# Attention steps in another order: VectorE's low part of the probabilities ahead of the maximum, ScalarE's high part ahead of the exponential

## The chip, the cores and the metric

The kernel runs on one core of a Trainium2 chip. The metric is the device time in microseconds (us) of one execution. TensorE (PE) multiplies matrices, VectorE (DVE) and ScalarE (ACT) work on elements and read PSUM banks, GpSimd (POOL) works on elements in SBUF, SyncE (SP) starts the transfers of the weights. Each engine runs its own instructions in the order in which they are written, and waits on semaphores for the others.

## What is computed

Two transformer blocks of two layers each, over 512 tokens of width 1024, in float32. The change is in the attention of the first block, which runs once in each of its two layers. There are 8 heads of grouped-query attention and 8 of latent attention (MLA). For each head:

```python
sc = jnp.einsum('bqhgd,bkhd->bhgqk', qblk, k).astype(jnp.float32) * scale
p = jax.nn.softmax(sc, axis=-1).astype(v.dtype)
return jnp.einsum('bhgqk,bkhd->bqhgd', p, v)
```

The queries and keys of an MLA head come from a small product of a latent vector, part of which is turned by a rotary embedding.

## The kernel before

Every float32 operand of a product is held as a high part (rounded to fp32r, names that end in H) and a low part (the rest, names that end in L), and each product is three matmuls: high by high, low by high, high by low (lines 1800, 1801 and 1802, in a helper). A matmul over 512 columns takes TensorE some 0.23 us from start to start.

The program is a list of steps. A planner appends them in order, and then each engine goes through the whole list and issues its own part of every step. So the order in the list is the order on every engine, and a step in which an engine has no part costs it nothing.

`attention_steps` writes the attention as a pipeline of 72 turns x. A unit is a tile of 128 queries of one head, 4 to a head, so 64 units a layer. In turn x the list holds these steps:

- att_scores of unit x: TensorE's scores (into bank 2 or 3), VectorE's negated row maximum (STAT<-bank, line 1494), ScalarE's exponential with its row sum (TMP<-bank, line 1174);
- att_normalise of unit x-1: VectorE's reciprocal of the sum (line 1499), GpSimd's multiplication of the 128x512 tile by it (line 883);
- att_transpose of unit x-3: four TensorE transposes (line 1961, into bank 4 or 5), ScalarE's high part of the transposed probabilities (PGH or PHH<-bank, line 1180);
- att_values: TensorE's product with the values, of a head whose four units are done;
- att_lo of unit x-4: VectorE's low part of the transposed probabilities (PGL or PHL<-bank, line 1388);
- then the steps that prepare the next heads (`latents`, turn_in, turn_high, turn_rest, turn_sine, turn_out, turn_low, mla_mm, mla_evac, mla_k, mla_v).

What ties the steps together: the transposes of unit x-3 wait for GpSimd's tile of x-3 and for the low part of unit x-5, which frees their bank. The scores of unit x wait for the exponential of x-2. The product with the values waits for the low parts of all four units of its head.

The preparation of an MLA head takes four turns (called phases here, after `(x + 2) % 4`). Phase 2: GpSimd multiplies by the cosine (FF<-FF, line 862) and cuts the key (MKL, line 873), after ScalarE's RH (line 1153) and MKH (line 1164). Phase 3: VectorE makes RL<-FF,RH (line 1388). Phase 0: TensorE turns it (lines 1915, 1916), VectorE multiplies by the sine (line 1475), GpSimd adds (FF<-FF, line 869), and TensorE makes the next head's product (mla_mm). Phase 1: ScalarE cuts MQH (line 1157) and VectorE MQL<-FF,MQH (line 1388), and for a head further on ScalarE makes MVH (line 1168) and VectorE MVL (line 1388). The rows call FF what is the tile of the head being prepared.

Of the kernel before, what the change touches and what calls it, by code (L numbers as in the profile page):

```python
# [29 lines left out]
KT = SEQ // P  # L30
# [151 lines left out]
def attention_steps(plan, latents):  # L182


    n = 2 * HEADS * KT
    mm = ev = None
    value_j = {}
    for x in range(n + 8):
        h, phase = divmod(x - KT - 4, KT)
        if 0 <= h < 2 * HEADS and phase == 3:  # L190
            plan.add("att_out_hi", h=h, pv=h)
        m_out, out_phase = divmod(x + 2 - (HEADS - 1) * KT, KT)
        if 1 <= m_out <= HEADS and out_phase == 1:
            plan.add("turn_out", **rotation)
            plan.add("turn_low", **rotation)
        if x < n:
            plan.add("att_scores", "u", h=x // KT, t=x % KT)
        if 1 <= x <= n:
            plan.add("att_normalise", u=x - 1)
        if 3 <= x <= n + 2:  # L200
            plan.add("att_transpose", u=x - 3, h=(x - 3) // KT, t=(x - 3) % KT)

        h, phase = divmod(x - KT - 4, KT)
        if 0 <= h < 2 * HEADS and phase < 3:
            plan.add("att_values", "pv" if phase == 2 else "", h=h, keys=((0, 1), (2,), (3,))[phase])
        if 4 <= x <= n + 3:
            plan.add("att_lo", u=x - 4, h=(x - 4) // KT, t=(x - 4) % KT)
        if 0 <= h < 2 * HEADS and phase == 3:
            plan.add("att_out_lo", h=h, pv=h)
        latents(x)  # L210

        m, phase = divmod(x + 2 - (HEADS - 1) * KT, KT)
        if 1 <= m <= HEADS and phase == 0:
            rotation["b"] = plan.add("turn", "b", **rotation).b
            plan.add("turn_sine", **rotation)
        if 0 <= m < HEADS and phase == 0:
            mm = plan.add("mla_mm", "c j:2", h=m, kt=[None])
            plan.cut_to(mm.c + 1)
        if 2 <= m <= HEADS + 1 and phase == 1:
            plan.add("mla_v", "b vh", h=m - 2, j=value_j[m - 2])  # L220
        if 0 <= m < HEADS and phase == 1:
            ev = plan.add("mla_evac", "rot mk", h=m, j=mm.j, done=mm.c)
            value_j[m] = mm.j
            rotation = dict(what="mla", h=m, rot=ev.rot, j=ev.j, rows=QK)
        if 0 <= m < HEADS and phase == 2:
            plan.add("turn_in", **rotation)
            plan.add("turn_high", **rotation)
            plan.add("mla_k", h=m, mk=ev.mk, j=ev.j)
        if 0 <= m < HEADS and phase == 3:
            plan.add("turn_rest", **rotation)  # L230
# [322 lines left out]
def build(nc, weights, x, layer_params, second_params, mats, tables, steps_t, s5_b, s5_c, out):  # L553
    ctx = ExitStack()
    with ctx:
# [179 lines left out]
        def probs(h):  # L735

            return (PGH[h % 2], PGL[h % 2]) if h < U_HEADS else (PHH[:, h % 2], PHL[:, h % 2])
# [331 lines left out]
        def _(act):  # L1069
# [36 lines left out]
            def step(l, st):  # L1106
                kind = st.kind
# [57 lines left out]
                elif kind == "mla_v":  # L1165
                    act.wait_ge(turn.sem, turn.after(l, st.b))
                    a = st.h % 2 * HD
                    act.activation(MVH[:, st.h % 2, :, a:a + HD], TURN[:].rearrange("p (k n) -> p k n", k=KT)[:, :, HD:P],
                                   ACT.Copy).then_inc(v_h.sem, 1)
                elif kind == "att_scores":  # L1170
                    act.wait_ge(row_max.sem, row_max.after(l, st.u))
                    act.wait_ge(probs_t.sem, probs_t.room(l, st.u))
                    r = st.u % 4
                    act.activation(TMP[:, r, :], BANK[2 + st.u % 2][:], ACT.Exp, bias=STAT[:, 0, r:r + 1],  # L1174
                                   accum_out=STAT[:, 1, r:r + 1]).then_inc(expd.sem, 1)
                elif kind == "att_transpose":
                    act.wait_ge(probs_t.sem, probs_t.after(l, st.u))
                    if st.u == KT * U_HEADS:
                        act.wait_ge(used.sem, used.after(l, LAST_ITEM.done))
                    act.activation(probs(st.h)[0][:, :, st.t * P:(st.t + 1) * P],  # L1180
                                   BANK[4 + st.u % 2][:].rearrange("p (k q) -> p k q", k=KT), ACT.Copy
                                   ).then_inc(probs_h.sem, 1)
                elif kind == "att_out_hi":
                    h, _, rows, k = pv_place(st.h)
                    act.wait_ge(pv.sem, pv.after(l, st.pv))
                    act.activation(h[rows, k, :], OUTB[rows, :], ACT.Copy).then_inc(y_h.sem, 1)
                elif kind in ("evac_ga", "evac_gb"):
                    b = kind == "evac_gb"
                    t = FF[:, 2 * b + st.m % 2, :]
                    act.wait_ge(bank_free.sem, bank_free.after(l, st.j))  # L1190
                    bias = G_BIAS + DT * b + st.m
                    act.activation(t, t, ACT.Sigmoid, bias=LP[:, l, bias:bias + 1]).then_inc(gate.sem, 1)
                elif kind == "merge":
                    act.wait_ge(merged.sem, merged.after(l, st.mg))
                    act.activation(MH[:, st.m, :], FF[:, 4 + st.m % 2, :], ACT.Copy).then_inc(merged_h.sem, 1)
                    if st.m == DT - 1:
                        act.preload_act_table_set(LOG_EXP)
                elif kind == "evac_ff" and st.group is not None:
                    act.wait_ge(bank_free.sem, bank_free.after(l, st.j))
                    if st.m == 0:  # L1200
                        act.activation(SQUARES[:], FF[:, st.m, :], ACT.Square).then_inc(first_sq.sem, 1)
                    elif st.a is not None:
                        square_for_pool(l, st.a, FF[:, st.m, :])
                    else:
                        square(l, st.s, FF[:, st.m, :])
                elif kind == "post":
                    factor(l, st.g, st.last_s, RCQ[:], 1.0 / DM, EPS)
                    to, norm, gain = next_norm(l, st)
                    for k in range(DT):
                        norm_tile(to, norm, k, gain)  # L1210
                elif kind == "evac_up":
                    act.wait_ge(bank_free.sem, bank_free.after(l, st.j))
                    act.activation(HH[:, st.m, :], TMP[:, 2 + st.m % 2, :], ACT.Square).then_inc(hid_h.sem, 1)  # L1213
# [1074 lines left out]
```

## Time and profile before

| what | value |
|---|---|
| time, median of 3 runs | 2993.85 us (2993.54 to 2993.94) |
| the profiled execution: own time, span | 2993.22 us, 2991.4 us |
| TensorE busy | 2829.0 us, 95% of the span |
| VectorE busy | 1614.9 us, 54% |
| ScalarE busy | 1147.8 us, 38% |
| GpSimd busy | 748.1 us, 25% |
| attention of the first layer, from the start of the span | about 57 to 270 us |
| attention of the second layer | about 865 to 1080 us |

The span runs from the first to the last instruction, and the execution's own time is 1.8 us longer. The shares are of the whole span. The attention is 14% of it, and there the engines other than TensorE have a larger share.

### The profile page before, as it was taken

What the parts mean: (1) busy time and instruction counts of PE and PEld (TensorE: products, weight loads), DVE (VectorE), ACT (ScalarE), POOL (GpSimd) and SP (SyncE); (2) the same over time, 40 slices, a digit from 0 to 9 for tenths busy, and PEclk for the clock granted to TensorE, in tenths of its full rate; (3) what the DMA queues carried; (4) which work ended last, traced back from release to release, by engine and by line L of the source; (5) the groups of instructions that cost most, each with busy time, mean ns of one, the idle gap of its engine ahead of it and who ended that gap; (6) DMA issues with size and microseconds to landing.
All of it is one profiled execution on the core that took longest, in us unless ns stands there. A gap on an engine that the chain in (4) does not pass through costs nothing.

```text
span 2991.4 us, 33731 instructions
## 1 busy us (share of the span) xinstructions
PE 2829.0 (95%) x12862; PEld 2317.4 (77%) x12862; DVE 1614.9 (54%) x2065; ACT 1147.8 (38%) x1758; POOL 748.1 (25%) x607
## 2 busy tenths in 40 slices
PE   8899999999998999999999967999999999999997
PEld 6677887888776778788887766878887789878886
DVE  5786446334367854453434895455533558555533
ACT  5675334222346753332223343322322348422221
POOL 2563113213025621140223161022200014122200
PEclk9999999999999999999999888999999989999999
DMA  3011322233220112223332201222232210123332
GB/s 136 28 43 43 99 92 85 94 97 99 85 85 22 43 53 95 85 92 99 99 95 87 79 19 60 92 92 95 96 106 99 83 52 1 57 92 99 99 103 88
DMA packets 75634, 236.68 MB, mean 79 GB/s; under 512 B 9776, under 2 KB 18240, under 8 KB 75488
## 3 DMA queue, kind: packets, MB, share of 16 engines
q1 hardware_dynamic: 74288, 231.31, 23.9%
q0 software_dynamic: 928, 3.27, 0.3%
q8 instruction: 103, 1.69, 0.2%
q14 instruction: 43, 0.35, 0.0%
q10 hardware_dynamic: 272, 0.06, 0.0%
HBM read 228.31 MB, written 2.10 MB: 77 GB/s over the span
## 4 chain that ended last, share of the span: by engine, by line
PE 86%; DVE 8%; ACT 2%; issue 1%; POOL 1%; DMA 1%; SPq 1%; DVEq 0%; POOLq 0%; ACTq 0%
PE bank L1800 27%; PE bank L1802 27%; PE bank L1801 27%; PE bank L2097 2%; PE bank L1961 1%; DVE S5S L1668 1%; DMA RAWW<-weights 1%; DVE STAT L1494 1%; PE bank L2003 1%; DVE S5S L1659 1%; SPq L817 1%; DVE WL L1383 1%; ACT WH L1072 1%; PE bank L1903 0%; DVE PHL L1388 0%
## 5 line engine op out<-in xcount | busy, mean ns | idle before, releaser
L1383 DVE TENSOR_TENSOR WL<-RAWW,WH 128x1024 fp32r<-128x1024 f32 (+2 forms) x424 | 573.7, 1357 | 862.5 <-ACT WH L1072 862.4
L1800 PE MATMUL bank<-UH,WH 128*128 128x512 f32 (+1 forms) x1920 | 762.3, 397 | 53.7 <-DVE UL L1393 29.4
L1801 PE MATMUL bank<-UL,WH 128*128 128x512 f32 (+1 forms) x1920 | 754.5, 393 | 0.0
L1802 PE MATMUL bank<-UH,WL 128*128 128x512 f32 (+1 forms) x1920 | 754.0, 393 | 0.0
L1072 ACT ACTIVATE WH<-RAWW 128x1024 fp32r<-128x1024 f32 (+2 forms) x424 | 433.9, 1027 | 368.5 <-DMA RAWW<-weights 368.0
L1800 PEld LDWEIGHTS bank<-UH,WH 128*128 128x128 f32 (+1 forms) x1920 | 364.6, 190 | 141.6 <-issue 58.1
L1801 PEld LDWEIGHTS bank<-UL,WH 128*128 128x128 f32 (+1 forms) x1920 | 365.0, 190 | 78.2 <-issue 2.4
L1802 PEld LDWEIGHTS bank<-UH,WL 128*128 128x128 f32 (+1 forms) x1920 | 364.4, 190 | 77.6
L1800 PE MATMUL bank<-HH,WH 128*128 128x512 f32 x512 | 199.2, 389 | 0.0
L1801 PE MATMUL bank<-HL,WH 128*128 128x512 f32 x512 | 199.2, 389 | 0.0
L1802 PE MATMUL bank<-HH,WL 128*128 128x512 f32 x512 | 199.2, 389 | 0.0
L883 POOL TENSOR_TENSOR TMP<-TMP,STAT 128x512 f32<-128x512 f32 x128 | 141.0, 1106 | 153.7 <-DVE STAT L1499 153.4
L893 POOL TENSOR_TENSOR TMP<-TMP 128x512 f32<-128x512 f32 x64 | 70.7, 1104 | 353.7 <-DVE TMP L1550 353.7
L1174 ACT ACTIVATE TMP<-bank,STAT 128x512 f32<-128x512 f32 x128 | 88.0, 687 | 133.1 <-DVE STAT L1494 131.0
L1800 PE MATMUL bank<-CHH,WH 128*128 128x512 f32 x352 | 137.2, 390 | 0.0
L1801 PE MATMUL bank<-CHL,WH 128*128 128x512 f32 x352 | 137.0, 389 | 0.0
L1802 PE MATMUL bank<-CHH,WL 128*128 128x512 f32 x352 | 136.9, 389 | 0.0
L1033 POOL TENSOR_TENSOR WTL<-SBW,WTH 128x1280 fp32r<-128x1280 f32 x16 | 47.1, 2944 | 348.9 <-ACT WTH L1340 348.9
L1213 ACT ACTIVATE HH<-TMP 128x512 fp32r<-128x512 f32 x64 | 40.4, 632 | 227.5 <-DVE TMP L1550 227.5
L1494 DVE TENSOR_REDUCE STAT<-bank 128x1 f32<-128x512 f32 x128 | 87.8, 686 | 51.0 <-PE bank L1802 50.8
L1800 PEld LDWEIGHTS bank<-HH,WH 128*128 128x128 f32 x512 | 96.1, 188 | 20.0
L1802 PEld LDWEIGHTS bank<-HH,WL 128*128 128x128 f32 x512 | 96.1, 188 | 19.9
(340 smaller groups left out, 4711.2 us busy)
## 6 DMA issues: line engine op xcount, KB each, us to landing
RAWW<-weights SPq DMA_DIRECT2D x424, 512.0 KB, 3.4
X<-x SPq DMA_DIRECT2D x8, 256.0 KB, 5.4
FF<-tables POOLq DMA_DIRECT2D x2, 1024.0 KB, 7.2
U<-S5U SPq DMA_DIRECT2D x16, 128.0 KB, 2.4
GEL<-U SPq DMA_DIRECT2D x128, 16.0 KB, 1.8
out<-FF SPq DMA_DIRECT2D x8, 256.0 KB, 2.0
S5B<-s_b POOLq DMA_DIRECT2D x1, 512.0 KB, 4.3
S5C<-s_c POOLq DMA_DIRECT2D x1, 512.0 KB, 4.3
```

What stands on the lines that cost most here:

```text
L883: pool.tensor_tensor(TMP[:, st.u % 4, :], TMP[:, st.u % 4, :], STAT[:, 2, st.u % 4:st.u % 4 + 1].to_broadcast([P, SEQ]), ALU.mult).then_in ...
L893: pool.tensor_tensor(TMP[:, st.m % 2, :], TMP[:, 2 + st.m % 2, :], TMP[:, 2 + st.m % 2, :], ALU.mult).then_inc(hid_f.sem, 1)
L1033: pool.tensor_tensor(WTL[st.h % 3][:], SBW[st.h % 3][:], f32(WTH[st.h % 3][:]), ALU.subtract).then_inc(w_l.sem, 1)
L1072: act.activation(slot_words(WH, c % SLOTS, size), slot_words(RAWW, c % SLOTS, size), ACT.Copy).then_inc(hi.sem, 1)
L1174: act.activation(TMP[:, r, :], BANK[2 + st.u % 2][:], ACT.Exp, bias=STAT[:, 0, r:r + 1], accum_out=STAT[:, 1, r:r + 1]).then_inc(expd.sem, 1)
L1213: act.activation(HH[:, st.m, :], TMP[:, 2 + st.m % 2, :], ACT.Square).then_inc(hid_h.sem, 1)
L1383: dve.tensor_tensor(slot_words(WL, c % SLOTS, size), slot_words(RAWW, c % SLOTS, size), f32(slot_words(WH, c % SLOTS, size)), ALU.subtract ...
L1494: dve.tensor_reduce(STAT[:, 0, r:r + 1], BANK[2 + st.u % 2][:], AX_X, ALU.max, negate=True).then_inc(row_max.sem, 1)
L1800: nc.tensor.matmul(out_, w[0], x_[0], start=start, stop=False, **how)
L1801: nc.tensor.matmul(out_, w[0], x_[1], start=False, stop=False, **how)
L1802: return nc.tensor.matmul(out_, w[1], x_[0], start=False, stop=stop, **how)
L2097: ins = nc.tensor.matmul(BANK[3 * (st.h % 2) + b][:, d:d + WIDE[k2]], mat, part[:, COL[k2]:COL[k2] + WIDE[k2]], start=False, stop=False, s ...
```

## The change

The step att_lo moves from behind the values to the front of its turn, ahead of VectorE's maximum. ScalarE's exponential gets a step of its own, att_exp, which stands behind att_transpose, so that the high part of unit x-3 comes ahead of the exponential of unit x. att_normalise stands behind both. No instruction is added or taken away, no wait is changed, and TensorE, GpSimd and SyncE issue the same instructions in the same order as before.

```diff
         if 1 <= m_out <= HEADS and out_phase == 1:
             plan.add("turn_out", **rotation)
             plan.add("turn_low", **rotation)
+        if 4 <= x <= n + 3:
+            plan.add("att_lo", u=x - 4, h=(x - 4) // KT, t=(x - 4) % KT)
         if x < n:
             plan.add("att_scores", "u", h=x // KT, t=x % KT)
+        if 3 <= x <= n + 2:
+            plan.add("att_transpose", u=x - 3, h=(x - 3) // KT, t=(x - 3) % KT)
+        if x < n:
+            plan.add("att_exp", u=x)
         if 1 <= x <= n:
             plan.add("att_normalise", u=x - 1)
-        if 3 <= x <= n + 2:
-            plan.add("att_transpose", u=x - 3, h=(x - 3) // KT, t=(x - 3) % KT)
 
         h, phase = divmod(x - KT - 4, KT)
         if 0 <= h < 2 * HEADS and phase < 3:
             plan.add("att_values", "pv" if phase == 2 else "", h=h, keys=((0, 1), (2,), (3,))[phase])
-        if 4 <= x <= n + 3:
-            plan.add("att_lo", u=x - 4, h=(x - 4) // KT, t=(x - 4) % KT)
         if 0 <= h < 2 * HEADS and phase == 3:
             plan.add("att_out_lo", h=h, pv=h)
         latents(x)
...
-                elif kind == "att_scores":
+                elif kind == "att_exp":
                     act.wait_ge(row_max.sem, row_max.after(l, st.u))
                     act.wait_ge(probs_t.sem, probs_t.room(l, st.u))
                     r = st.u % 4
```

VectorE in an MLA head, phases 1 and 2, before: MQL, then maximum (TENSOR_REDUCE), reciprocal, low part (PHL) of phase 1, YBL (low part of a head's result), MVL, then maximum, reciprocal, low part of phase 2.

```order
L1388 TENSOR_TENSOR MQL_75<-FF_58,MQH_74 96x512
L1494 TENSOR_REDUCE STAT_167<-bank3 128x1
L1499 RECIPROCAL STAT_167<-STAT_167 128x1
L1388 TENSOR_TENSOR PHL_57<-bank5,PHH_56 128x4x128
L1388 TENSOR_TENSOR YBL_81<-bank6,YBH_80 64x512
L1388 TENSOR_TENSOR MVL_79<-bank7,MVH_78 128x4x64
L1494 TENSOR_REDUCE STAT_167<-bank2 128x1
L1499 RECIPROCAL STAT_167<-STAT_167 128x1
L1388 TENSOR_TENSOR PHL_57<-bank4,PHH_56 128x4x128
```

The same place with the change (all line numbers behind the edit are 2 higher):

```order
L1390 TENSOR_TENSOR MQL_75<-FF_58,MQH_74 96x512
L1390 TENSOR_TENSOR PHL_57<-bank5,PHH_56 128x4x128
L1496 TENSOR_REDUCE STAT_167<-bank3 128x1
L1501 RECIPROCAL STAT_167<-STAT_167 128x1
L1390 TENSOR_TENSOR YBL_81<-bank6,YBH_80 64x512
L1390 TENSOR_TENSOR MVL_79<-bank7,MVH_78 128x4x64
L1390 TENSOR_TENSOR PHL_57<-bank4,PHH_56 128x4x128
L1496 TENSOR_REDUCE STAT_167<-bank2 128x1
L1501 RECIPROCAL STAT_167<-STAT_167 128x1
```

Each low part has moved ahead of its turn's maximum and reciprocal, the first of them to a place right behind MQL, the second right behind MVL.

ScalarE at the same place, before: MQH, then exponential (TMP) and high part (PHH) of phase 1, MVH and the two evacuations of the next head, and exponential and high part of phase 2.

```order
L1157 ACTIVATE MQH<-FF 96x512
L1174 ACTIVATE TMP,STAT<-bank,STAT 128x512
L1180 ACTIVATE PHH<-bank 128x4x128
L1168 ACTIVATE MVH<-bank 128x4x64
L1129 ACTIVATE FF<-bank 96x512
L1131 ACTIVATE KVF<-bank 128x512
L1174 ACTIVATE TMP,STAT<-bank,STAT 128x512
L1180 ACTIVATE PHH<-bank 128x4x128
L1153 ACTIVATE RH<-FF 96x512
```

And with the change:

```order
L1159 ACTIVATE MQH<-FF 96x512
L1182 ACTIVATE PHH<-bank 128x4x128
L1176 ACTIVATE TMP,STAT<-bank,STAT 128x512
L1170 ACTIVATE MVH<-bank 128x4x64
L1131 ACTIVATE FF<-bank 96x512
L1133 ACTIVATE KVF<-bank 128x512
L1182 ACTIVATE PHH<-bank 128x4x128
L1176 ACTIVATE TMP,STAT<-bank,STAT 128x512
L1155 ACTIVATE RH<-FF 96x512
```

The high part and the exponential of each turn have changed places, so MVH and RH now stand directly behind an exponential.

## Rows read from the trace of the kernel before

**Rows 1.** Stretches: length, busy us of PE, PEld, DVE, ACT, POOL; PEclk, DMA.

```profile
100.00:150.00 50.00, 42.69 (x194) 32.06 (x194) 41.30 (x69) 31.80 (x70) 32.02 (x30) 0.93 0.06 21
125.00:130.00 5.00, 1.60 (x6) 1.53 (x7) 5.00 (x8) 2.30 (x5) 2.49 (x3) 0.78 0.00 0
200.00:250.00 50.00, 47.83 (x243) 36.31 (x241) 41.32 (x73) 35.82 (x80) 33.35 (x28) 1.00 0.13 43
```

**Rows 2.** Waits of PE in 55 to 285 us: total, times, longest.

```profile
PE bank L1961 <- DVE PGL L1388: 4.7, 3, 3.9
PE bank L1961 <- DVE PHL L1388: 4.6, 5, 2.9
```

**Rows 3.** Timeline of VectorE: start us, duration us; [idle before <- releaser].

```profile
203.92 0.68 DVE L1494 TENSOR_REDUCE STAT<-bank 128x1 f32<-128x512 f32 x1
...
212.84 0.69 DVE L1388 TENSOR_TENSOR MQL<-FF,MQH 96x512 fp32r<-96x512 f32 x1 [0.18 <-ACT MQH L1157]
213.45 0.68 DVE L1494 TENSOR_REDUCE STAT<-bank 128x1 f32<-128x512 f32 x1
...
214.12 0.67 DVE L1388 TENSOR_TENSOR PHL<-bank,PHH 128x512 fp32r<-128x512 f32 x1
...
215.74 0.42 DVE L1388 TENSOR_TENSOR MVL<-bank,MVH 128x256 fp32r<-128x256 f32 x1 [0.23 <-ACT MVH L1168]
216.08 0.68 DVE L1494 TENSOR_REDUCE STAT<-bank 128x1 f32<-128x512 f32 x1
```

**Rows 4.** Timeline of ScalarE, same stretch.

```profile
205.79 0.62 ACT L1153 ACTIVATE RH<-FF 96x512 fp32r<-96x512 f32 x1
...
214.17 0.69 ACT L1174 ACTIVATE TMP<-bank,STAT 128x512 f32<-128x512 f32 x1 [1.43 <-DVE STAT L1494]
...
214.85 0.59 ACT L1180 ACTIVATE PHH<-bank 128x512 fp32r<-128x512 f32 x1
215.32 0.38 ACT L1168 ACTIVATE MVH<-bank 128x256 fp32r<-128x256 f32 x1
```

**Rows 5.** Timeline of GpSimd, same stretch.

```profile
204.75 1.04 POOL L883 TENSOR_TENSOR TMP<-TMP,STAT 128x512 f32<-128x512 f32 x1 [1.59 <-DVE STAT L1499]
205.75 1.29 POOL L862 TENSOR_TENSOR FF<-FF 96x512 f32<-96x512 f32 x1
207.01 1.81 POOL L873 TENSOR_TENSOR MKL<-KVF,MKH 64x512 fp32r<-64x512 f32 x1
208.79 2.03 POOL L883 TENSOR_TENSOR TMP<-TMP,STAT 128x512 f32<-128x512 f32 x2
210.79 1.28 POOL L869 TENSOR_TENSOR FF<-FF 96x512 f32<-96x512 f32 x1
```

**Rows 6.** Timeline of VectorE: maxima of phase 2, first and last of six.

```profile
179.21 0.68 DVE L1494 TENSOR_REDUCE STAT<-bank 128x1 f32<-128x512 f32 x1
...
241.02 0.68 DVE L1494 TENSOR_REDUCE STAT<-bank 128x1 f32<-128x512 f32 x1
```

**Rows 7.** Timeline of VectorE and GpSimd around an RL.

```profile
219.29 1.72 DVE L1388 TENSOR_TENSOR RL<-FF,RH 96x512 fp32r<-96x512 f32 x1
...
220.42 1.48 POOL L883 TENSOR_TENSOR TMP<-TMP,STAT 128x512 f32<-128x512 f32 x1
```

**Rows 8.** Timeline of VectorE, GpSimd and PE around the longest wait.

```profile
123.40 3.59 DVE L1444 SCALAR_TENSOR_TENSOR CF<-CF,LP,RCQ 128x512 f32<-128x512 f32 x1
...
123.95 1.27 POOL L869 TENSOR_TENSOR FF<-FF,KVF 128x512 f32<-128x512 f32 x1
...
125.18 1.27 POOL L880 TENSOR_TENSOR CL<-CF,CH 128x512 fp32r<-128x512 f32 x1
126.92 0.68 DVE L1494 TENSOR_REDUCE STAT<-bank 128x1 f32<-128x512 f32 x1
...
127.59 0.67 DVE L1388 TENSOR_TENSOR PGL<-bank,PGH 128x512 fp32r<-128x512 f32 x1
...
128.40 1.09 PE L1961 MATMUL bank<-MAT,TMP 128*128 128x128 f32 x4 [3.93 <-DVE PGL L1388]
```


## The prediction

> **What bounds the kernel now.** I read the stretches first, then TensorE's waits, then the timelines of the engines that it waits for. TensorE is busy 47.8 of 50 us from 200 to 250 us, in the MLA heads, and 42.7 of 50 between 100 and 150, where the grouped heads and the latents overlap [rows 1]. So at most 2 us in 50 can be won late, and 7 early. The reader should see in the list of waits that TensorE's transposes wait for a low part, the very instruction that moves: 4.7 us in 3 waits for PGL and 4.6 us in 5 for PHL in one layer, of which 3.9 and 2.9 us are one wait each [rows 2]. The rest, 9.3 - 6.8 = 2.5 us, is six short ones.
>
> The short waits in the MLA stretch don't tell what sets the pace there. The timelines do, if one follows the chain backwards. From the maximum of phase 2 at 203.92 [rows 3], GpSimd's multiplication starts at 204.75, after an idle time that ended with VectorE's reciprocal; then GpSimd runs without a gap: 862 at 205.75, 873 at 207.01, two 883 from 208.79, 869 at 210.79 [rows 5]. MQL follows at 212.84, the maximum of phase 1 right behind it at 213.45 [rows 3], the exponential at 214.17 (ScalarE had waited 1.43 us for the maximum), the high part at 214.85, MVH at 215.32 [rows 4], MVL at 215.74, and the next maximum of phase 2 at 216.08 [rows 3]. This is a closed loop over VectorE, GpSimd and ScalarE of 216.08 - 203.92 = 12.16 us a head, with no slack but the hand-overs. The six maxima of phase 2 from 179.21 to 241.02 [rows 6] are five loops of 61.81 / 5 = 12.36 us on average: some are longer, because an RL that GpSimd held up (1.72 us [rows 7], where the like MQL takes 0.69 [rows 3]) delays TensorE's turn and its scores by a few tenths. TensorE's own work in a head is less than the loop: 12.36 x 47.83 / 50 = 11.8 us [rows 1]. So TensorE looks like the bound (96%), and the loop is.
>
> **The change, part by part.** Instructions, waits and transfers are the same; only places on VectorE and ScalarE move.
>
> Low part first, where it waits for room: the transposes of a turn get their bank when the low part ends. Before, it came behind a maximum and a reciprocal. In the longest wait VectorE came free at 126.92, did the maximum and reciprocal, began the low part at 127.59, and TensorE started at 128.40 [rows 8]. With the low part at 126.92 TensorE starts 0.67 us earlier. There are two such waits per layer, so 1.3 us. Of the six short ones (2.5 us) I take some 1.0 us, since those in the MLA heads are inside the loop and save nothing by themselves. Gain: 2.3 us a layer, 4.6 us in all. Bounds: nothing (the time turns up at the next wait), and 9.3 x 2 = 18.6 us if all these waits went.
>
> Low part first, in the loop: VectorE spends 0.60 to 0.61 us on a PSUM-sourced tile from start to start (212.84 to 213.45; the low part at 214.12 lasts 0.67 with its tail [rows 3]). The loop passes VectorE's turn at two places, phase 1 (MQL, then maximum) and phase 2 (MVL, then maximum). At both the low part now stands between, and what it works on has long been there. Cost: 2 x 0.60 us. Queued behind: the maximum and exponential of that turn, the reciprocal, and GpSimd's whole row of five.
>
> High part ahead of the exponential: MVH no longer waits for the high part, 215.32 - 214.85 = 0.47 us [rows 4], which the loop wins back, for the high part's transposes end before the later exponential can start, so it fits into ScalarE's idle time (1.43 us there). In phase 2 RH likewise moves up by 0.47 us and back by 0.60. Were that cover gone, the exponential would wait up to 0.59 us for a high part.
>
> Together: loop 12.16 + 1.20 - 0.47 = 12.9 us, against 12.36 now: +0.53 us on five loops, and the last pass, with the full 0.73, because there TensorE has no product to hide it behind. That is 3.4 us a layer, 6.7 in all. Lower bound: nothing, if the long loops absorb it (12.36 against a loop that TensorE ends at 11.8); upper: 6 x 0.73 x 2 = 8.8 us.
>
> Sum, against the execution with the rows: 2993.2 - 4.6 + 6.7 = 2995.3 us. The median of the runs is 0.6 above that execution, so 2995.9 us.
>
> **A price that no row gives.** RL reads two SBUF tiles. After the change it can start at: maximum of phase 2, +0.71 exponential, +0.68 RH, +0.62 and hand-over, so 2.06 us behind the maximum, while 862 runs from 1.83 to 3.09 [rows 3 to 5]. Now it happens to come at 3.08, just as 862 ends. What the rows show of such a wait differs: at 219.29 RL was let in between 873 and 883 (883 took 1.48 us in place of 1.04) [rows 7]; but CF, at 123.40, stayed shut out over two boundaries, 883 to 869 and 869 to 880, and took 3.59 us [rows 8]. If RL is let in behind 862, it ends at 3.6, not later than needed, and costs nothing; if it waits for one more instruction, 873, it starts at 4.2, the next reciprocal comes at 6.05 (low part, maximum and 0.60 to the reciprocal behind it), and that delays 883 and 869 by 0.43 us a loop, 0.43 x 6 x 2 = 5 us. The upper end is worked out below. I take the lower end, as RL's own rows, not CF's, are the nearest: it was let in at the first boundary.
>
> The Trainium skill (GPSIMD Engine Reference, Key points) says that GpSimd shares its SBUF interfaces with VectorE, with contention for instructions with two SBUF inputs. The trace agrees: RL and CF are stretched [rows 7, 8], and the PSUM-sourced low parts take 0.67 us [rows 3, 8]. It says nothing on who goes first, and by it the moved low parts cost 0.60 us each at any place, while RL is the one at risk.
>
> **The rivals.**
> 1. *RL shut out until GpSimd rests* (slower). It would wait for 862, 873 and one 883, to 5.2 us behind the maximum; then RL, low part, maximum (3 x 0.60), the reciprocal and 883 (0.23 + 1.0), 869 and MQH (1.32), MQL (0.73): MQL at 10.3 where it is at 8.92 now. The loop is then 12.9 + 1.4 = 14.3, which is 1.9 more than now, over seven RLs a layer: 27 us in place of 6.7. Time 3016 us. For it: CF's row; against: RL's. It decides once RL loses the boundary behind 873.
> 2. *CF gets in early* (faster). The low part ahead of the maximum also lets CF ask 0.6 us sooner, at 122.8, in an 862. If it is let in behind that 862, the long wait of 3.93 us shrinks to some 0.4 and the low clock that follows it (PEclk 0.78 [rows 1]; four transposes took 1.09 us [rows 8]) goes too, for some 1.2 us. That is 3.5 + 1.2 - 0.7 = 4.0 us a layer more: 2988 us. For it: the row of RL again; against: CF's own, and that the earlier steps may shift GpSimd as well.
> 3. *The loop isn't binding* (faster). If the extra 0.73 us falls into slack that I don't see, 6.7 us drop out: 2989 us; with rival 2, 2981.
> 4. *RL waits for one instruction more*: 2995.9 + 5 = 3001 us.
>
> **How the numbers follow.** My forecast, 2995.9, own range 2991 to 3001: 0.40. Rival 1: 0.17. Rival 2: 0.18. Rival 3: 0.14. Rival 4: 0.11. A measurement here can tell about 0.2%, 6 us, from no change: faster is below 2987.9, slower above 2999.8. Faster: two thirds of rival 2, 0.12, a good half of rival 3, 0.08, and 0.02 of my own case, 0.22. Slower: rival 1, 0.17, most of rival 4, 0.08, and 0.06 of my own, 0.31. Same: 0.47. The range runs from 2983 (below it only rivals 2 and 3 together) to 3012 (above it most of rival 1).
>
> **What would show it.** Right: the maxima of phase 2 stand 12.9 us apart, with no idle time between MQL, low part and maximum; MVH follows the exponential by 0.68; TensorE's longest wait for PGL is 3.2 in place of 3.9 us; the short waits for PHL are gone, and waits for MQL or RL grow. RL's duration tells the rivals: about 1.6 us is my case, 2.9 rival 4, over 3.5 rival 1. Wrong: maxima less than 12.4 us apart, or a CF under 1.3 us at this place.

## The result and the profile after

| | before | after |
|---|---|---|
| median | 2993.47 us (2991.56 to 2993.94, 6 runs) | 3005.18 us (3001.07 to 3008.47, 6 runs) |
| ratio, 95% interval | | 1.0036 [1.0026, 1.0047] |
| profiled execution, span | 2991.4 us | 3002.4 us |
| TensorE busy | 2829.0 us | 2831.1 us |

The change costs 11.7 us, 0.4%. That is within the predicted range, and above the 2995.9 us of the forecast. Line numbers in the kernel after are two higher than in the rows of before: 883 is 885, 862 is 864, 873 is 875, 869 is 871, 880 is 882. The kernels below have them up to nine higher. The stretches of [rows 1], in the kernel after:

```profile
100.00:150.00 50.00, 45.07 (x195) 33.55 (x196) 41.53 (x68) 30.94 (x69) 32.42 (x30) 0.90 0.05 17
200.00:250.00 50.00, 45.49 (x232) 35.17 (x231) 45.04 (x69) 34.74 (x76) 30.41 (x27) 1.00 0.14 43
```

From 200 to 250 us TensorE (the second number) is busy 45.5 of 50 us, where it was 47.8. The MLA heads have become slower. From 100 to 150 us it is busy 45.1 us, where it was 42.7, but for about as many instructions (195 for 194), at a granted clock of 0.90 in place of 0.93 of the full one. TensorE's own waits in the first layer's attention (55 to 285 us), to set beside [rows 2]:

```profile
PE bank L1917 <- DVE RL L1390: 6.3, 8, 1.0
PE bank L1802 <- DVE YBL L1390: 3.3, 6, 1.5
...
PE bank L1963 <- DVE PHL L1390: 2.2, 1, 2.2
PE bank L1963 <- DVE PGL L1390: 1.6, 1, 1.6
```

The transposes' short waits for low parts are gone, as the change intends: one wait for PHL in place of five, one for PGL in place of three. In their place TensorE waits 8 times for RL, 6.3 us in all; before, it waited for RL once:

```profile
PE bank L1915 <- DVE RL L1388: 1.0, 1, 1.0
```

VectorE over one head shows why, to set beside [rows 3]:

```profile
217.21 0.42 DVE L1390 TENSOR_TENSOR MVL<-bank,MVH 128x256 fp32r<-128x256 f32 x1 [0.32 <-ACT MVH L1170]
217.55 0.68 DVE L1390 TENSOR_TENSOR PHL<-bank,PHH 128x512 fp32r<-128x512 f32 x1
218.15 0.68 DVE L1496 TENSOR_REDUCE STAT<-bank 128x1 f32<-128x512 f32 x1
...
220.20 2.86 DVE L1390 TENSOR_TENSOR RL<-FF,RH 96x512 fp32r<-96x512 f32 x1
222.98 0.68 DVE L1390 TENSOR_TENSOR PHL<-bank,PHH 128x512 fp32r<-128x512 f32 x1
...
227.46 0.69 DVE L1390 TENSOR_TENSOR MQL<-FF,MQH 96x512 fp32r<-96x512 f32 x1 [0.19 <-ACT MQH L1159]
228.07 0.68 DVE L1390 TENSOR_TENSOR PHL<-bank,PHH 128x512 fp32r<-128x512 f32 x1
228.67 0.68 DVE L1496 TENSOR_REDUCE STAT<-bank 128x1 f32<-128x512 f32 x1
...
230.47 0.42 DVE L1390 TENSOR_TENSOR MVL<-bank,MVH 128x256 fp32r<-128x256 f32 x1 [0.47 <-ACT MVH L1170]
```

GpSimd in the same head, to set beside [rows 5]:

```profile
218.98 1.04 POOL L885 TENSOR_TENSOR TMP<-TMP,STAT 128x512 f32<-128x512 f32 x1 [1.70 <-DVE STAT L1501]
219.98 1.29 POOL L864 TENSOR_TENSOR FF<-FF 96x512 f32<-96x512 f32 x1
221.23 1.28 POOL L875 TENSOR_TENSOR MKL<-KVF,MKH 64x512 fp32r<-64x512 f32 x1
222.47 1.49 POOL L885 TENSOR_TENSOR TMP<-TMP,STAT 128x512 f32<-128x512 f32 x1
224.40 1.04 POOL L885 TENSOR_TENSOR TMP<-TMP,STAT 128x512 f32<-128x512 f32 x1 [0.45 <-DVE STAT L1501]
225.40 1.29 POOL L871 TENSOR_TENSOR FF<-FF 96x512 f32<-96x512 f32 x1
```

From MVL to MVL is 13.26 us. The two low parts stand between MVL and its maximum and between MQL and its maximum, each with 0.60 us from start to start. RL is issued at 220.20, while 864 runs. It doesn't get in when 864 ends at 221.27. It gets in when 875 ends at 222.51, and the 885 behind it is stretched from 1.04 to 1.49 us. The row of GpSimd behind RL waits for it in turn: it is idle for 0.45 us ahead of the next 885, until the reciprocal that stands behind RL. The six RLs from 180.43 to 246.94, and their six in the second layer, all take 2.85 or 2.86 us. This is what the prediction called rival 4: "RL's duration tells the rivals: about 1.6 us is my case, 2.9 rival 4".

**Where the 11 us are.** Three starts on VectorE mark each layer's attention: its first maximum, the first MVL and the last MVL. In the first layer they stand at 57.18, 178.87 and 261.83 us before, at 57.13, 177.44 and 266.54 after; in the second at 865.37, 987.28 and 1070.44 before, at 870.83, 991.87 and 1080.20 after. Up to the first MVL the two layers take 121.69 and 121.91 us before, 120.31 and 121.04 after: 2.3 us won. From the first to the last MVL, which is seven heads, they take 82.96 and 83.16 before, 89.10 and 88.33 after: 11.3 us lost. That makes 9.1 us. The rest of the span took 2581.7 us before and 2583.6 after, and from 2581.7 to 2588.2 us in the profiled executions of the fourteen kernels here. The kernels are alike in it, but for the last turns of each attention: from the last MVL to the last YBL it is 8.9 us in each layer before and 8.8 after. So one execution's span can't tell a difference of some 5 us, and below I go by the medians and by these stretches.

**One stall with two outcomes.** The scaling of the latent (CF, [rows 8]) is issued at the same distance to GpSimd's row in both layers of the profiled execution. VectorE in the first and in the second layer:

```profile
122.00 2.40 DVE L1446 SCALAR_TENSOR_TENSOR CF<-CF,LP,RCQ 128x512 f32<-128x512 f32 x1
...
935.70 4.76 DVE L1446 SCALAR_TENSOR_TENSOR CF<-CF,LP,RCQ 128x512 f32<-128x512 f32 x1
```

GpSimd in the first layer and then in the second:

```profile
121.48 1.29 POOL L864 TENSOR_TENSOR FF<-FF 96x512 f32<-96x512 f32 x1
122.73 1.04 POOL L885 TENSOR_TENSOR TMP<-TMP,STAT 128x512 f32<-128x512 f32 x1
123.73 1.80 POOL L871 TENSOR_TENSOR FF<-FF,KVF 128x512 f32<-128x512 f32 x1
...
935.18 1.29 POOL L864 TENSOR_TENSOR FF<-FF 96x512 f32<-96x512 f32 x1
936.43 1.04 POOL L885 TENSOR_TENSOR TMP<-TMP,STAT 128x512 f32<-128x512 f32 x1
937.43 1.26 POOL L871 TENSOR_TENSOR FF<-FF,KVF 128x512 f32<-128x512 f32 x1
938.65 1.26 POOL L882 TENSOR_TENSOR CL<-CF,CH 128x512 fp32r<-128x512 f32 x1
```

In the first layer CF gets in between 885 and 871, and 871 is stretched to 1.80 us. In the second it gets in nowhere until GpSimd rests at 939.91. TensorE's longest wait for PGL is 1.6 us in the first layer and 4.0 in the second. Yet the second layer is only 0.73 us longer up to its first MVL: its low part starts 2.35 us later behind CF and it is 2.8 us behind at 954.03, but from there to 965.5 us the first layer waits longer for TensorE and ScalarE. So the length of a CF isn't its price.

### The profile page after: what moved, and what is told of

It reads as the page before. It is cut to its first block, busy times and chain, and to the rows that moved or that the text cites. A ratio compares the mean times of both kernels' runs of the same rounds, so it can differ in the third digit from the quotient of the medians.

```text
span 3002.4 us, 33731 instructions
## 1 busy us (share of the span) xinstructions
PE 2831.1 (94%) x12862; PEld 2321.3 (77%) x12862; DVE 1634.7 (54%) x2065; ACT 1149.1 (38%) x1758; POOL 750.4 (25%) x607
## 4 chain that ended last, share of the span: by engine, by line
PE 81%; DVE 11%; ACT 3%; issue 2%; POOL 2%; DMA 1%; SPq 1%; DVEq 0%; POOLq 0%; ACTq 0%
PE bank L1802 26%; PE bank L1804 25%; PE bank L1803 25%; PE bank L2099 2%; DVE RL L1390 1%; DVE S5S L1670 1%; DVE STAT L1496 1%; DVE PHL L1390 1%; DMA RAWW<-weights 1%; PE bank L2005 1%; DVE S5S L1661 1%; PE bank L1963 1%; SPq L819 1%; POOL FF L871 1%; ACT WH L1074 0%
## 5 line engine op out<-in xcount | busy, mean ns | idle before, releaser
L1803 PEld LDWEIGHTS bank<-HL,WH 128*128 128x128 f32 x512 | 96.1, 188 | 20.0
```

What stands on the lines that cost most here:

```text
L1803: nc.tensor.matmul(out_, w[0], x_[1], start=False, stop=False, **how)
```

## The experiments

Two theories stood at the start; each expectation below numbers its own theories 1 and 2 again. Theory 1: the loss is in the loop of an MLA head, two low parts of 0.60 us and an RL that is shut out. Theory 2: the loss, or a part of it, comes from ScalarE's new order. The kernel before had its median at 2993.9 us in the comparison of the four kernels that stand behind "after" in this table, at 2994.9 in that of the next four, 2995.6 in that of the next three and 2996.0 in that of the last; each ratio is to its own comparison. The stretches are those marked above, both layers added. They come from one execution of each kernel, and for the kernel with the late key cut and for the changed order from turn 24 it is the slowest of its runs (3006.28 us and 3010.64 us):

| kernel | median us | ratio, 95% interval | to first MVL | first to last MVL |
|---|---|---|---|---|
| before | 2993.5 | | 243.6 | 166.1 |
| after | 3005.2 | 1.0036 [1.0026, 1.0047] | 241.4 | 177.4 |
| low part alone | 3042.1 | 1.0160 [1.0146, 1.0174] | 253.0 | 203.2 |
| high part alone | 2995.7 | 1.0007 [0.9998, 1.0016] | 243.3 | 167.1 |
| after, low part late in phases 1, 2 | 2992.6 | 0.9991 [0.9982, 1.0000] | 240.9 | 166.2 |
| after, key cut late | 2998.7 | 1.0019 [1.0010, 1.0028] | 246.4 | 171.9 |
| after's order up to turn 23 | 2996.9 | 1.0005 [0.9996, 1.0014] | 245.0 | 166.5 |
| after's order from turn 24 | 3007.8 | 1.0038 [1.0025, 1.0052] | 243.3 | 177.9 |
| after, low part late in phase 2 | 2994.2 | 0.9998 [0.9989, 1.0007] | 235.0 | 172.0 |
| low part late in 1, 2, and key cut late | 2989.5 | 0.9979 [0.9970, 0.9988] | 240.8 | 164.2 |
| before, CF ahead of the sine product | 2991.3 | 0.9986 [0.9977, 0.9995] | 239.2 | 165.8 |
| the one of 2989.5, and ckv0's low part later | 2987.6 | 0.9975 [0.9964, 0.9986] | 238.3 | 163.4 |
| after, two latents' low parts later | 3002.3 | 1.0022 [1.0013, 1.0031] | 237.6 | 177.5 |
| before, key cut late, ckv0's low part later | 2996.3 | 1.0004 [0.9995, 1.0013] | 241.5 | 166.5 |

**The two halves of the change.** The first kernel moves only the low part to the front (below; exponential and high part stay as before), the second only the exponential, with the normalisation, behind the transposes:

```diff
+        if 4 <= x <= n + 3:
+            plan.add("att_lo", u=x - 4, h=(x - 4) // KT, t=(x - 4) % KT)
         if x < n:
             plan.add("att_scores", "u", h=x // KT, t=x % KT)
...
-        if 4 <= x <= n + 3:
-            plan.add("att_lo", u=x - 4, h=(x - 4) // KT, t=(x - 4) % KT)
```

> Half of the change: the low part ahead of the maximum, ScalarE's order as before. Theory 1 (a loop over VectorE, GpSimd and ScalarE sets the pace of the MLA heads, the low part stands in it twice, and RL, asked for during 862, is shut out until 873 is done): the loop keeps the high part ahead of MVH, so the maxima of phase 2 stand 13.25 + 0.47 = 13.7 us apart (13.25 with the whole change), RL is still shut out, and the time is 3008 to 3012 us. Theory 2 (ScalarE's order is what costs: the exponential waits for the transposes): the time is that of before, 2993 us, or less by the transposes' waits.

Measured: 3042.13 us. The sign was right, the size was not: four times the whole change. VectorE in one head of it:

```profile
216.65 0.69 DVE L1388 TENSOR_TENSOR PHL<-bank,PHH 128x512 fp32r<-128x512 f32 x1 [1.26 <-ACT PHH L1180]
...
217.92 2.62 DVE L1388 TENSOR_TENSOR RL<-FF,RH 96x512 fp32r<-96x512 f32 x1
```

The low part now stands ahead of the maximum and waits 1.26 us for its high part, which ScalarE makes only behind the exponential of the turn before. The maximum, and all that waits for it, waits too. The loop (MVL to MVL) is 14.7 to 15.7 us. So the two halves of the change belong together: I had priced the high part ahead of the exponential as a gain of 0.47 us a loop, but with the low part in front it saves 1.8 us a loop (the six loops of the first layer take 15.1 us on average, 13.3 in the changed kernel).

> The other half: the high part ahead of the exponential, the low part where it was. Theory 1: the loop loses the high part ahead of MVH, 12.16 - 0.47 = 11.7 us, so TensorE's own 11.8 us or its wait for RL sets the pace; maxima of phase 2 11.9 to 12.2 us apart, 2987 to 2992 us. Theory 2: the loss of the whole change is here, 3002 to 3006 us.

Measured: 2995.74 us, loops of 12.3 us on average as before. Neither theory's number came. ScalarE's order alone costs nothing that can be told, and wins nothing: theory 2 falls. Why the 0.47 us that it should free wins nothing isn't shown. In one head of it the maximum behind that of phase 2 waits 0.80 us for TensorE's scores (218.81), and RL takes 1.4 to 1.6 us in all twelve heads, where before every other one took 0.68.

**The low part, phase by phase.** The changed kernel, with the low part at its old place in phases 1 and 2 (below), and then in phase 2 alone:

```diff
-        if 4 <= x <= n + 3:
+        if 4 <= x <= n + 3 and (x + 2) % 4 not in (1, 2):
             plan.add("att_lo", u=x - 4, h=(x - 4) // KT, t=(x - 4) % KT)
...
+        if 4 <= x <= n + 3 and (x + 2) % 4 in (1, 2):
+            plan.add("att_lo", u=x - 4, h=(x - 4) // KT, t=(x - 4) % KT)
```

> The whole change, but in phases 1 and 2 (the two places where the loop passes VectorE's turn) the low part stays behind the maximum. Theory 1: the loop is free of low parts and of the high part, so the maxima of phase 2 are under 12.2 us apart, and the time is 2985 to 2991 us, faster than before. A theory in which early low parts cost at any place predicts half of the loss back, some 2999 us.

> The changed kernel, but in phase 2 alone the low part stays behind the maximum, as before. Theory 1, each low part ahead of a maximum in the loop costs its own 0.60 us: loops of 12.65 us in place of 13.25, RL still 2.86 us since it asks at the same distance behind the maximum of phase 2, 3005 - 12 x 0.6 = 2998 us. Theory 2, only the blocked RL sets the loop: loops of 13.2 us and 3005 us.

Measured, phases 1 and 2: 2992.55 us, 1.6 us above what was expected, with loops of 12.2 us. Phase 2 alone: 2994.16 us. VectorE in one loop of the latter:

```profile
211.16 0.42 DVE L1392 TENSOR_TENSOR MVL<-bank,MVH 128x256 fp32r<-128x256 f32 x1 [0.32 <-ACT MVH L1172]
...
214.03 2.38 DVE L1392 TENSOR_TENSOR RL<-FF,RH 96x512 fp32r<-96x512 f32 x1
...
223.82 0.42 DVE L1392 TENSOR_TENSOR MVL<-bank,MVH 128x256 fp32r<-128x256 f32 x1 [0.47 <-ACT MVH L1172]
```

The loop is 12.66 us, 0.60 less than 13.26, by one low part less, while RL is shut out up to the same boundary: it asks 0.48 us later behind the maximum and takes 0.48 us less. That is theory 1's term. The six loops of a layer won 3.6 us by it, but the seventh, short one grew by 0.6 and 1.2 us, so the stretch from the first to the last MVL won 5.4 us in all, not 7.2. The kernel won more than its 7 us because it also won 6.4 us up to the first MVL, where the CFs of cq2 took 1.15 and 1.16 us.

Its two layers differ there: up to the first MVL the first takes 116.11 us and the second 118.87, 2.8 us more. Two instructions on VectorE differ: QL, which starts at the same distance from the layer's first maximum in both, and CF of ckv1 behind it:

```profile
128.05 0.67 DVE L1392 TENSOR_TENSOR QL<-FF,QH 128x512 fp32r<-128x512 f32 x1
...
132.43 0.72 DVE L1448 SCALAR_TENSOR_TENSOR CF<-CF,LP,RKV 128x512 f32<-128x512 f32 x1
...
934.49 2.52 DVE L1392 TENSOR_TENSOR QL<-FF,QH 128x512 fp32r<-128x512 f32 x1
...
940.72 3.35 DVE L1448 SCALAR_TENSOR_TENSOR CF<-CF,LP,RKV 128x512 f32<-128x512 f32 x1
```

Together they are 4.5 us longer in the second layer, and 1.7 us of that is gone at once, because VectorE waits 1.70 us for ScalarE's QH in the first layer alone (136.12).

**RL let in.** The changed kernel, with the key's cut (MKH on ScalarE, MKL on GpSimd) behind RL's step, so that an 883 and not 873 follows 862 (in their own numbers 885, 875 and 864); and the same together with the late low parts of phases 1 and 2:

```diff
-            plan.add("mla_k", h=m, mk=ev.mk, j=ev.j)
         if 0 <= m < HEADS and phase == 3:
             plan.add("turn_rest", **rotation)
+            plan.add("mla_k", h=m, mk=ev.mk, j=ev.j)
```

> The whole change, with mla_k (ScalarE's MKH and GpSimd's 873) moved from phase 2 to phase 3, behind RL, so that 862 is followed by 883 and not by 873. Theory 1, RL let in behind 862: RL takes 1.6 us in place of 2.86, the maxima stand 12.9 us apart in place of 13.25, and the time is some 5 us less than with the change, 3000 us. If RL is shut out there as well, nothing changes, 3005 us. A theory in which GpSimd's hold on RL is the whole cause predicts the time of before, 2993 us.

> The changed kernel with the low part late in phases 1 and 2, and the key's cut on GpSimd (862) behind RL's step, so that GpSimd's next instruction at RL is a product of the probabilities. Theory 1, the loop of 12.79 us that the late key cut alone left goes to 11.6 by the two low parts of 0.60 us, below TensorE's own 11.8 us a head, so TensorE sets the pace: maxima and MVL 11.9 us apart, 2986 to 2990 us. Theory 2, with the low parts late RL meets GpSimd's row at another place and loses a boundary again (RL over 2 us), or the key's low half comes late for the scores: 2992 to 2996 us.

The key's cut is line 873 of before, not 862 as the last expectation writes.

Measured, the first: 2998.65 us. VectorE:

```profile
221.95 1.63 DVE L1390 TENSOR_TENSOR RL<-FF,RH 96x512 fp32r<-96x512 f32 x1
```

GpSimd:

```profile
221.74 1.29 POOL L864 TENSOR_TENSOR FF<-FF 96x512 f32<-96x512 f32 x1
222.98 1.49 POOL L885 TENSOR_TENSOR TMP<-TMP,STAT 128x512 f32<-128x512 f32 x1
```

RL is issued 0.21 us into 864, as in the changed kernel, and here it is let in when 864 ends. Its steady loops are 12.78 to 12.80 us, where the prediction's own case had 12.9, and its heads lose 5.7 us, where that case had 6.7. The difference to 13.26 is what the shut-out RL costs: 0.47 us a loop, predicted 0.43. All of it stands in GpSimd's row: from the first 885 to 871 it takes 5.95 us (220.74 to 226.69), in the changed kernel 6.42 (218.98 to 225.40). Ahead of the first MVL it takes 5 us more than the changed kernel in this execution, with CF of cq2 at 4.76 us in both layers. The medians don't show that: they are 6.5 us apart the other way, and this execution was 7.6 us above its own median.

The second: 2989.50 us, faster than before. Its six loops take 12.1 us on average, not the 11.9 expected. RL is shut out over one product in nine of the twelve heads (1.9 us), as the second theory has it, but that this makes the difference isn't shown. The time is the first theory's. Without either low part the loop is 0.67 us shorter than 12.79, not 1.20: the two don't come back in full. What holds the loop then (TensorE's own 11.8 us a head, or RL) isn't shown.

**First stretch or heads.** The changed order only in turns 0 to 23, and only from turn 24 on (the condition of the second is x >= 24; each step is added at its old place where it doesn't hold):

```diff
+        early = x < 24
```

> The changed order (low part first, high part ahead of the exponential) only in turns 0 to 23, where the grouped heads and the latents are; the order of before from turn 24 on, so in all of the MLA heads. Theory 1, the prediction's gain term is real: transposes that waited for a low part start earlier, 4.6 us of the two layers come back, so 2989 us against 2994, and the MLA heads repeat every 12.4 us with RL at 1.1 to 1.7 us. Theory 2, the gain turns up again at the next wait or the high part's earlier place costs as much: 2993 to 2996 us. If CF of cq2 takes 4.7 us here too, this stretch alone carries the spread of the changed kernel's times: runs several us apart.

> The complement: the order of before in turns 0 to 23, the changed order from turn 24 on. Theory 1, the loss is all in the MLA heads and is larger than the net result, because the first stretch wins 4.6 us: loops of 13.25 us with RL at 2.86 us, 2994 + 16 = 3010 us. Theory 2, nothing is won in the first stretch: 3005 us, the same loops. In both the sum of the two complements' differences is the 11.3 us of the whole change, if the stretches add up.

Measured: 2996.94 us and 3007.82 us. All of the loss is in the MLA heads (177.9 - 166.1 = 11.8 us), with the same loops and RLs as in the changed kernel. By their medians the two halves lose 2.1 and 12.9 us, 15 in all, where the whole change loses 11.7; whether they don't add up or this is noise, the intervals don't say. The first stretch by itself is 1.4 us longer than before, so the prediction's gain isn't there; nor in the medians, where the interval allows 1.2 us won at most. VectorE at the long wait, in the kernel with the changed order up to turn 23:

```profile
122.24 4.77 DVE L1453 SCALAR_TENSOR_TENSOR CF<-CF,LP,RCQ 128x512 f32<-128x512 f32 x1
126.93 0.68 DVE L1397 TENSOR_TENSOR PGL<-bank,PGH 128x512 fp32r<-128x512 f32 x1
```

CF asks 1.16 us sooner than in [rows 8], and comes through at 127.01, where it was 126.99. The low part does begin right behind it, 0.66 us earlier than before, but the maximum behind it begins at 127.53, 0.61 us later. What VectorE won ahead of CF, it spent waiting for GpSimd.

**CF by itself.** In the kernel before, in turn 18, CF one instruction earlier on VectorE, ahead of the sine product:

```diff
-    (17, "turn", "q3"), (17, "turn_in", "kr"), (17, "latent_high", "cq1"), (18, "turn_sine", "q3"), (18, "turn_high", "kr"),
-    (18, "latent_low", "cq1"), (18, "latent", "cq2"), (19, "turn_out", "q3"), (19, "turn_rest", "kr"), (19, "latent_high", "cq2"),
+    (17, "turn", "q3"), (17, "turn_in", "kr"), (17, "latent_high", "cq1"), (18, "latent", "cq2"), (18, "turn_sine", "q3"), (18, "turn_high", "kr"),
+    (18, "latent_low", "cq1"), (19, "turn_out", "q3"), (19, "turn_rest", "kr"), (19, "latent_high", "cq2"),
```

> The kernel before, with one swap on VectorE in turn 18: the scaling of the latent (CF of cq2) ahead of the sine product (KVF), so that it asks 0.6 us sooner, at the start of a product of GpSimd or just before it. Theory 1, the long wait of TensorE for PGL (3.9 us) is CF shut out behind three instructions of GpSimd, and costs its length: let in at once or at the first boundary, CF takes 0.7 to 1.6 us, the wait falls under 1.5 us and two layers win 5 to 6 us, 2988 us. Theory 2, the wait is made by the chain of maximum, product and transposes, not by CF: the wait stays over 3 us whatever CF takes, and the time is 2994 us. If CF is shut out here too it takes 4.5 to 5 us and the time is 2994 to 2997 us, which says nothing against theory 1.

Measured: 2991.27 us. VectorE there:

```profile
124.26 1.73 DVE L1444 SCALAR_TENSOR_TENSOR CF<-CF,LP,RCQ 128x512 f32<-128x512 f32 x1
```

GpSimd:

```profile
123.15 1.29 POOL L862 TENSOR_TENSOR FF<-FF 96x512 f32<-96x512 f32 x1
124.40 1.04 POOL L883 TENSOR_TENSOR TMP<-TMP,STAT 128x512 f32<-128x512 f32 x1
126.74 1.27 POOL L869 TENSOR_TENSOR FF<-FF,KVF 128x512 f32<-128x512 f32 x1 [1.30 <-DVE KVF L1475]
```

TensorE's waits from 100 to 150 us:

```profile
PE bank L1961 <- DVE PGL L1388: 2.5, 2, 2.1
```

CF is shut out over one 883, and then GpSimd has to wait for the sine product and rests, so CF takes 1.73 us in place of 3.59, 1.86 less. The wait shrinks from 3.9 to 2.1 us, by as much: that part of it was CF's. The wait didn't fall under 1.5 us, and the kernel won 4.4 us, by the marks 4.4 up to the first MVL, not 5 to 6. This swap of two instructions is better than the kernel before, by more than its interval.

Next, GpSimd's low part of a latent (line 880, in these kernels 884 or 882), for whose end CF waits, one turn later: for ckv0 (below) in the fastest kernel so far, and for cq1 and ckv0 in the changed kernel:

```diff
-    (21, "latent_high", "ckv0"), (22, "turn_out", "kr"), (22, "latent_low", "ckv0"), (22, "latent", "ckv1"), (23, "turn_low", "kr"),
-    (23, "latent_high", "ckv1"), (24, "latent_low", "ckv1")]
+    (21, "latent_high", "ckv0"), (22, "turn_out", "kr"), (22, "latent", "ckv1"), (23, "turn_low", "kr"),
+    (23, "latent_low", "ckv0"), (23, "latent_high", "ckv1"), (24, "latent_low", "ckv1")]
```

> The kernel with low parts late in phases 1 and 2 and the late key cut, and GpSimd's low part of the latent ckv0 (884) one turn later, behind the product of turn 23. CF of ckv1 then has GpSimd to itself once the product (887) that it meets ends: 2.2 us at most in place of 3.36, and TensorE's wait for PHL there 1.7 us in place of 2.9. Theory 1 (a shut-out lasts until GpSimd rests, if it isn't let in before): 2989.5 - 2.3 = 2987 us. Theory 2 (CF's place behind GpSimd's row isn't what TensorE waits for): 2989.5 us, wait 2.9 us.

> The changed kernel, with GpSimd's low parts of the latents cq1 and ckv0 one turn later, so that GpSimd's row of three behind each of the two CFs is one shorter. The loops of the MLA heads stay at 13.25 us with RL at 2.86 us. Theory 1, the spread of the changed kernel's times (3001 to 3008.5 us) is CF of cq2 that is let in after two boundaries (2.40 us) or only when GpSimd rests (4.76 us): it now takes 2.4 to 3.6 us and CF of ckv1 2.3, the runs lie within 3 us of each other, at 3000 to 3002 us. Theory 2, the spread is from elsewhere: runs still 5 us or more apart.

Measured, the first: 2987.63 us. TensorE's waits from 100 to 150 us:

```profile
PE bank L1965 <- DVE PHL L1392: 4.7, 3, 1.7
```

CF of ckv1 takes 2.12 us and the wait for PHL is 1.7 us in place of 2.9, both as expected. This is the fastest kernel of the study; whether it is faster than the one it was made from the intervals don't say. The second: 3002.30 us (3000.58 to 3005.51). Its CFs are steady in both layers (3.55 and 0.73 us), but its runs still lie 5 us apart. So the spread of the changed kernel isn't shown to come from CF; I had thought that it was.

**The control.** The order of before, with only the two moves on GpSimd (key cut, low part of ckv0 one turn later):

> The control of the best kernel so far (2987.6 us against 2995.6 in its own comparison): the order of before for low parts and exponentials, with only the two moves on GpSimd (key cut behind RL's step, low part of the latent ckv0 in turn 23). Theory 1, the win of the best kernel came from GpSimd's row and needs nothing of the change: within 1.5 us of it, ratio to before 0.9975. Theory 2, half of it came from CF of cq2 being let in after 1.16 us, which the early low parts of phases 0 and 3 brought about: here that CF still takes 3.6 us, TensorE waits 3.9 us for PGL, only CF of ckv1 is shorter (2.1 us, 1.1 us a layer), ratio 0.999.

Measured: 2996.34 us. Its theory 1 falls: the moves on GpSimd alone win 1.7 us by the marks, and nothing that the medians tell. Of its theory 2 the mechanism is there, VectorE at the long wait:

```profile
123.44 3.56 DVE L1444 SCALAR_TENSOR_TENSOR CF<-CF,LP,RCQ 128x512 f32<-128x512 f32 x1
```

CF of cq2 is shut out as before, where the early low parts of phases 0 and 3 let it in at 1.16 us, and TensorE waits 3.9 us for PGL. CF of ckv1 takes 1.81 us, and with it the control wins 1 us a layer up to the first MVL, as expected; but the expected ratio of 0.999 lies just outside the measured interval, 0.9995 to 1.0013. To the best kernel it lacks 3.2 us in the first stretch, which I put down to this CF, and 3.1 in the heads. So, by the marks, more than half of what the best kernel wins (8.0 us, the control 1.7) rests on a part of the change.

## Why the prediction was right and where it failed

The range held the time, and the side, slower by over 0.2%, was given 0.31. The range was 29 us wide. What happened is rival 4, which I gave 0.11, and not my own case: the median lies outside its range of 2991 to 3001. It also lies 4 us above the 3001 of rival 4, which may be the gain of 4.6 us that rival 4 kept and that came at half at most.

- *The loop of an MLA head binds, and each low part in it costs 0.60 us*: right for the changed kernel. With RL let in the loop was 12.79 us, predicted 12.9; the low part of phase 2 out of it gave 13.26 to 12.66. That the loop also set the pace before isn't shown: with 0.47 us taken out of it by the high part alone it stayed at 12.3 us. TensorE's share fell to 45.5 of 50 us, which rules out rival 3.
- *"If RL is let in behind 862, it ends at 3.6 ... I take the lower end, as RL's own rows, not CF's, are the nearest"*: this step failed. RL was shut out over 873 (875 in the kernel after) in the twelve heads with a steady loop. I had taken RL's own rows as the near ones because they are RL's, and the place in GpSimd's row differed: in the steady heads of before RL was issued just as 862 ended (207.00 against 207.01, where 873 starts [rows 5]) or one tenth of a us later, CF in the middle of a row of GpSimd [rows 8], and the change moved RL to such a place. The term that I left out as zero, 5 us, measured 0.47 x 12 = 5.6.
- *Cost 6.7 us*: 5.7 us with RL let in. With rival 4's 5 us it is 11.7, and 11.3 were measured between the first and the last MVL.
- *Gain 4.6 us*: failed in size. 2.3 us in the marks of the profiled execution, and nothing in the kernel that has the changed order in this stretch alone. The low part did move up behind CF, by 0.66 us there. But the other move, which I had listed as a help at most (CF asks sooner), made CF wait longer by what it came sooner.
- *High part ahead of the exponential, worth 0.47 us a loop*: mis-sized both ways, nothing alone and 1.8 us a loop once the low part stands in front. "What it works on has long been there" was true only through this half of the change. I should have priced the low part's wait in each phase against ScalarE's order.
- *Rival 2, CF gets in early*: a part of it came, in the first layer of the profiled execution, where CF got in behind 885, not behind 864 (2.40 us); that layer won 1.4 us up to the first MVL, not 4 us more than forecast, and the second, with CF at 4.76, 0.9.

## What to carry to other kernels

Where VectorE takes two tiles from SBUF while GpSimd has a row of instructions with no gap, take the whole row as the upper bound of its price, not the rows where it happened to be let in; a move of a few hundredths of a us can decide. A gap helped here: a swap of two instructions, after which GpSimd itself has to wait, was worth 0.14%. A step that is moved ahead to free a buffer must be looked at from the engine that it now blocks: the 0.60 us in front of the maximum of phase 2 came back in full as loop time, and a step without its producer moved along with it cost four times the whole change. And a part of a change can be worth keeping where the whole is not: low parts early in two phases of four, with the two moves on GpSimd, came out 0.25% faster than before.

## What the runs showed of the hardware

A VectorE instruction with two SBUF inputs that meets GpSimd's row came out in three ways. It waited for the end of GpSimd's instruction and then ran: RL took 1.63 us. It then lost to one or more of GpSimd's next instructions as well: RL took 2.86 us with one lost, CF 4.76 with three. Or it wasn't held up at all. In the kernel before, VectorE and GpSimd:

```profile
130.63 0.68 DVE L1388 TENSOR_TENSOR QL<-FF,QH 128x512 fp32r<-128x512 f32 x1
131.23 0.74 DVE L1444 SCALAR_TENSOR_TENSOR CF<-CF,LP,RKV 128x512 f32<-128x512 f32 x1
...
130.20 2.67 POOL L883 TENSOR_TENSOR TMP<-TMP,STAT 128x512 f32<-128x512 f32 x1 [1.41 <-DVE STAT L1499]
```

The GpSimd instruction that is held up by VectorE shows it by its own length: 885 of 1.49 us, 871 of 1.80, this 883 of 2.67. The Trainium skill (SBUF — State Buffer, SBUF: two separate sides) states that, of a VectorE instruction with two SBUF inputs and a GpSimd instruction that reads SBUF, the one that "starts first gets the pair for the whole instruction; the other fully blocks". The rows agree in that 864 keeps its 1.29 us when RL comes 0.22 us into it. By the starts in the trace they don't agree in two places: the 883 above starts at 130.20, ahead of QL and CF, and was the one that waited; and RL stands in the changed kernel's rows from 220.20, 875 begins at 221.23, and 875 went first. Whether the start of a record is the moment that counts, no run here shows.

The outcome at a place is sharp, and it nearly always repeats. In the three kernels with late low parts in phases 1 and 2, RL comes late in the cosine product (866, which is 862 of before). The 26 RLs issued 0.92 to 0.97 us behind its start lost to the next instruction (1.86 to 2.14 us), the 10 issued 0.98 or 0.99 us behind it won (0.84 or 0.85 us), and that whether the next was the key's cut or a product of the probabilities. One of each, from the kernel in which nothing but these low parts differs from the changed kernel, VectorE and then GpSimd:

```profile
229.96 2.14 DVE L1392 TENSOR_TENSOR RL<-FF,RH 96x512 fp32r<-96x512 f32 x1
...
242.60 0.84 DVE L1392 TENSOR_TENSOR RL<-FF,RH 96x512 fp32r<-96x512 f32 x1
...
229.02 1.28 POOL L866 TENSOR_TENSOR FF<-FF 96x512 f32<-96x512 f32 x1
...
241.61 1.28 POOL L866 TENSOR_TENSOR FF<-FF 96x512 f32<-96x512 f32 x1
```

The long CF of [rows 8] was as close a case. Over the fourteen traces, the 20 CFs issued 0.42 or 0.43 us into a product of the probabilities of 1.04 us, with the next instruction right behind it, were let in at its end and took 1.16 us. The 6 issued 0.45 to 0.49 us into it lost two boundaries and took 3.56 to 3.59 us; the one of [rows 8] is the nearest of them. In the kernel with the low part alone CF came 0.43 us into an 883 with the same 869 behind it, and took 1.16 us. One place doesn't repeat: of the six CFs issued 0.51 or 0.52 us into the cosine product with the same row behind it, in three kernels, five took 4.75 to 4.77 us and one 2.40.

What decides stays open. It isn't how late in GpSimd's instruction VectorE asks: RL issued 0.21 or 0.22 us into 864 won at its end when 885 was next (12 of 12) and lost when 875 was next (36 of 36, in three kernels), RL issued 0.80 to 0.84 us into it won with 875 next (6 of 6) and lost with 885 next (2 of 2). I know of no rule that fits all of these.
